# Level products of a chunked decay and of a triangular inverse on 64 of 128 columns

## The chip, the cores and the metric

The program runs on one core of a Trainium2 chip. The metric is the device time of one execution in microseconds (us); three executions were timed. TensorE multiplies 128x128 stationary weights with moving columns and writes to PSUM; VectorE and ScalarE read PSUM and SBUF; GpSimd computes only a few small powers; the sync engine issues the weight transfers. In the rows TensorE's matmuls are PE, its weight loads PEld, VectorE is DVE, ScalarE is ACT.

## The reference, cut to what matters

Two layers of a first block (attention, the HGRN2 recurrence, memory attention), then two layers of a second block (gated delta rule, pooling, retention, then a feed-forward part), on 256 positions of width 1024, all in fp32. The change touches two computations. In the first block, the decayed scores of the recurrence:

```
A = jnp.cumsum(lfc, axis=2)
diff = A[:, :, :, None, :] - A[:, :, None, :, :]
decay = jnp.exp(jnp.where(causal[:, :, None], diff, -jnp.inf))
scores = jnp.einsum('bhtd,bhtsd,bhsd->bhts', qc, decay, kc)
```

In the second block, the solution with a unit lower triangular matrix in the gated delta rule:

```
m = jnp.where(strict, jnp.einsum('bhnid,bhnjd->bhnij', k_beta, k) * decay, 0.0)
a = m + jnp.eye(CHUNK, dtype=m.dtype)
...
sol = lax.linalg.triangular_solve(a, rhs, left_side=True, lower=True, unit_diagonal=True)
```

## The kernel before, in words

Nothing schedules the work: each engine runs a list of instructions written out by hand, with semaphores between the lists. The 256 positions are two tiles `t` of 128 rows; both computations have four heads of width 128.

**Weights.** Every weight matrix is cut into units of up to four 128-row slices of 512 columns. A unit arrives by a transfer into one of four slots; ScalarE rounds it in two parts of 128x1024 (`round_weights`, line 1007), VectorE subtracts the rounded part from the original (`weight_rests`, line 1368), and TensorE multiplies with both (`split_part`, lines 548 and 557): 24 matmuls of 512 columns for a unit. `round_until(i)` and `rests_until(i)` in the lists of ScalarE and VectorE say at which place the units up to number i are prepared. TensorE's list puts one such unit between two steps of the small computations.

**Steps.** All small products go through the four PSUM banks `mp` in one fixed order of steps (`ORDER_1`, `ORDER_2`). A step waits until the bank's last content was read (`begin`), raises `step_done`, and its reader raises `step_read`.

**Decayed scores (first block).** Per layer `hg_level(n)` computes for n = 0 to 8 and each tile four fp32 products, one for each head (line 668). For n from 1 to 7 the level stands for pairs of neighbouring runs of m = 2^(n-1) positions, and only entries whose row is in a left run and whose column is in the right run of the same pair count. VectorE's `products(n)` fills only the left runs of `kmul` and the right runs of `qmul`; ScalarE's `level_exp(n)` (lines 1073 and 1074) gives the exponentials. `collect(n)` on VectorE copies 128x512 from PSUM into `hst` under the level's mask (line 1621). TensorE's order is: level n, one weight unit, level n+1.

**Inverse (second block).** The inverse `inv` of a head's 128x128 matrix and its transpose `invT` are built level by level, m = `LEVELS[n]` = 2, 4, ..., 64 for n = 1 to 6. VectorE masks the level's part `ml` out of the matrix (`level_mask`, raises `inv_ready`). Then, for each tile and head (`quad`, line 826):

- Y = ml^T inv, copied by ScalarE into `yl` (`evacuate`, lines 1238 and 1291);
- Z = invT^T yl, which VectorE subtracts from `inv` (line 1896; not at the last level);
- W = yl^T invT, which VectorE subtracts from `invT` (line 1900).

All operands are 128x128 for each head, though a level changes only the left runs of m columns of `inv` and the right runs of `invT`. TensorE's order at a level is: Y of both tiles, one weight unit, Z of both tiles, W of both tiles, one weight unit, then what `BETWEEN` puts there (retention and pooling). ScalarE's list at the start of this stage (lines 1287 to 1311) is: take over the sums of the `DZ` unit, sigmoid of `RG`, sigmoid of `DZ`, two roundings of the next unit, the two copies of Y1, two more roundings.

```
for n, g in enumerate(("DZ", "G2", "G3", "G4", "G5", "G0", None)):
    if n < 6:
        round_until(17 + 2 * n)
    for t in range(TT if n > 0 else 0):
        evacuate(f"Y{n}_{t}", yl[:, t], bank(s(f"Y{n}_{t}"), NH, P))
```

Beside these, `attn_values` (line 722) multiplies 128x128 weights with 64 moving columns, the step `ba` (line 789) with 16, and `pool_mix` (line 872) with 256.

## Time and profile before

| | |
|---|---|
| time, median of 3 | 1568.52 us (1568.07 to 1570.97) |
| the profiled execution's own time | 1567.28 us |
| its span in the trace | 1565.5 us |
| mean granted clock of TensorE | 0.976 |
| busy: PE, PEld, DVE, ACT, POOL | 1464.9, 1228.0, 954.9, 694.9, 52.9 us |
| first block, level products | 86.6 to 140.9 us, and 344.1 to 398.3 us |
| second block, inverse | 644.6 to 765.9 us, and 1162.5 to 1283.4 us |

The span lies 1.8 us inside the time of its own execution, and that execution 1.2 us below the median of the three. Matmuls are pipelined: a busy figure of PE holds overlapping pieces, so how long a matmul holds the engine is read from the chain of waits or from the distance of the starts. An fp32 matmul of this program stands in the trace as two records, a product with rounded operands (line 548, 557, 789) as one. The granted clock is a share of 2.4 GHz; its two levels are 1.0 and 0.5.

### The profile page before, as it was taken

The page shows a single profiled execution, that of the slowest core. Times are in us where ns is not written, and L with a number is a line of the kernel's source. Part 1 is how long each engine was busy: PE and PEld are TensorE (multiplying, and loading weights), DVE is VectorE, ACT ScalarE, POOL GpSimd, SP SyncE. Part 2 cuts the span into 40 slices and gives each one's busy share as a digit, 9 for nine tenths or more (in the row PEclk, how much of TensorE's full clock was granted, in tenths as well). Part 3 has the DMA queues.
Part 4 walks back from the last instruction along what each step waited for, and adds up shares of the span by engine and source line. Part 5 has one row for each costly group of instructions (what it writes and reads, how often), then busy time and mean ns, then how long its engine had stood idle before and what let it go on. Part 6 is the DMA issues. An engine that isn't in the chain of part 4 may idle for free.

```text
span 1565.5 us, 19971 instructions
## 1 busy us (share of the span) xinstructions
PE 1464.9 (94%) x8234; PEld 1228.0 (78%) x8234; DVE 954.9 (61%) x1160; ACT 694.9 (44%) x971; POOL 52.9 (3%) x41
## 2 busy tenths in 40 slices
PE   5999878999887999999998999989999999899997
PEld 4988757888776798888554999869888866489986
DVE  7588553779763657955344566464796543366654
ACT  4754563575553457433204443344754311343332
POOL 0002000000200000000000000000000000000000
PEclk9999888999998999999999999999999999999999
DMA  7444222544322365433343565544543334445553
GB/s 257 145 152 152 72 98 81 173 151 149 121 86 77 132 208 178 135 108 108 108 161 108 188 187 178 188 147 169 188 135 108 108 108 162 134 152 179 181 176 120
DMA packets 138985, 225.79 MB, mean 144 GB/s; under 512 B 7888, under 2 KB 54288, under 8 KB 138768
## 3 DMA queue, kind: packets, MB, share of 16 engines
q1 hardware_dynamic: 133456, 221.60, 43.1%
q10 hardware_dynamic: 5440, 2.93, 0.6%
q8 instruction: 66, 1.08, 0.3%
q14 instruction: 23, 0.19, 0.0%
HBM read 223.46 MB, written 1.05 MB: 143 GB/s over the span
## 4 chain that ended last, share of the span: by engine, by line
PE 84%; DVE 7%; ACT 5%; issue 2%; POOL 1%; ACTq 0%; DMA 0%; POOLq 0%; DVEq 0%
PE gp L557 42%; PE gp L548 20%; PE gp L530 5%; PE mp L826 5%; PE gp L607 3%; PE mp L512 2%; PE mp L668 2%; DVE wt_rest L1368 2%; DVE arena L1362 1%; ACT arena L1081 1%; PE mp L722 1%; POOL rs_out L2023 1%; ACT first_hi L1007 1%; ACT arena L1238 0%; PE mp L789 0%
## 5 line engine op out<-in xcount | busy, mean ns | idle before, releaser
L1368 DVE TENSOR_TENSOR wt_rest<-wt,wt_hi 128x1024 fp32r<-128x1024 f32 x140 | 164.9, 1221 | 72.1 <-ACT wt_hi L1007 72.0
L1007 ACT ACTIVATE wt_hi<-wt 128x1024 fp32r<-128x1024 f32 x140 | 140.3, 1051 | 116.7 <-DMA wt<-in_ffn_down 60.5
L1368 DVE TENSOR_TENSOR wt_rest<-wt,mix_hi 128x1024 fp32r<-128x1024 f32 x112 | 132.5, 1221 | 56.4 <-ACT mix_hi L1007 55.6
L1368 DVE TENSOR_TENSOR wt_rest<-wt,first_hi 128x1024 fp32r<-128x1024 f32 x118 | 139.2, 1219 | 41.2 <-ACT first_hi L1007 40.5
L548 PE MATMUL gp<-hT_hi,wt_hi 128*128 128x256 f32 x576 | 163.3, 284 | 0.0
L548 PE MATMUL gp<-hT_hi,wt_rest 128*128 128x256 f32 x576 | 163.0, 283 | 0.0
L548 PE MATMUL gp<-hT_rest,wt_hi 128*128 128x256 f32 x576 | 163.0, 283 | 0.0
L557 PE MATMUL gp<-wt_rest,mix_hT_hi 128*128 128x512 f32 x384 | 153.8, 400 | 0.0
L1007 ACT ACTIVATE first_hi<-wt 128x1024 fp32r<-128x1024 f32 x118 | 121.1, 1062 | 71.4 <-PE gp L557 60.4
L557 PE MATMUL gp<-mix_hi,mix_hT_hi 128*128 128x512 f32 x352 | 142.6, 405 | 8.6 <-DVE arena L1785 5.7
L1007 ACT ACTIVATE mix_hi<-wt 128x1024 fp32r<-128x1024 f32 x112 | 114.7, 1059 | 79.5 <-PE gp L557 29.8
L557 PE MATMUL gp<-mix_hi,mix_hT_rest 128*128 128x512 f32 x352 | 137.9, 392 | 0.0
L980 ACT ACTIVATE arena<-gp 128x1024 f32<-128x1024 f32 x48 | 49.1, 1022 | 168.7 <-PE gp L557 168.7
L1362 DVE TENSOR_TENSOR arena<-arena,gp 128x512 f32<-128x512 f32 (+1 forms) x56 | 44.9, 801 | 124.4 <-ACT arena L1339 68.1
L557 PE MATMUL gp<-first_hi,first_hT_hi 128*128 128x512 f32 x256 | 105.3, 411 | 6.9 <-DVE wt_rest L1368 6.9
L548 PEld LDWEIGHTS gp<-hT_rest,wt_hi 128*128 128x128 f32 x576 | 110.6, 192 | 0.0
L548 PEld LDWEIGHTS gp<-hT_hi,wt_hi 128*128 128x128 f32 x576 | 110.5, 192 | 0.0
L548 PEld LDWEIGHTS gp<-hT_hi,wt_rest 128*128 128x128 f32 x576 | 110.5, 192 | 0.0
L1238 ACT ACTIVATE arena<-mp 128x512 f32<-128x512 f32 x84 | 46.2, 601 | 131.6 <-PE mp L826 61.3
L557 PE MATMUL gp<-wt_rest,first_hT_hi 128*128 128x512 f32 x256 | 103.8, 406 | 0.0
L2023 POOL TENSOR_TENSOR rs_out<-rs_in,minus_half 128x1 f32<-128x1 f32 (+3 forms) x37 | 52.7, 1426 | 1506.5 <-DVE rs_in L1373 1506.5
L557 PE MATMUL gp<-first_hi,first_hT_rest 128*128 128x512 f32 x256 | 103.0, 402 | 0.0
(290 smaller groups left out, 3086.3 us busy)
## 6 DMA issues: line engine op xcount, KB each, us to landing
wt<-in_w_in SPq DMA_DIRECT2D x100, 1024.0 KB, 5.0
wt<-in_ffn_gate SPq DMA_DIRECT2D x44, 512.0 KB, 4.0
wt<-in_ffn_up SPq DMA_DIRECT2D x44, 512.0 KB, 5.0
wt<-in_w_out SPq DMA_DIRECT2D x20, 1024.0 KB, 5.0
wt<-in_ffn_down SPq DMA_DIRECT2D x20, 1024.0 KB, 5.0
wt<-in_w_mem_kv SPq DMA_DIRECT2D x8, 1024.0 KB, 5.1
wt<-in_w_branch_pool SPq DMA_DIRECT2D x4, 1024.0 KB, 5.1
wt<-in_w_branch_ret SPq DMA_DIRECT2D x4, 1024.0 KB, 5.0
```

The lines of the kernel that those rows point to most:

```text
L512: last = nc.tensor.transpose(bank(step)[:, P * j:P * j + P], tile, ident)
L530: last = nc.tensor.matmul(group_bank(group, t), stationary(k0 + k, t), wt[:, u % SLOTS, k, :], start=(k0 + k == 0), stop=(k0 + k == GROUPS ...
L548: last = nc.tensor.matmul(o, a[:, k, P * c:P * c + P], b[:, :, k0 + k, :], start=(k0 + k == 0 and c % 2 == 0 and i == 0), stop=(k0 + k == ...
L557: last = nc.tensor.matmul(group_bank(group, t), a, b[:, k, :], start=(kk == k_first and i == 0), stop=(kk == k_last and i == 2))
L607: last = nc.tensor.matmul(group_bank(GROUPS[g][0], t), stationary(k0 + k, t), wt[:, u % SLOTS, k, :], start=(k0 + k == 0), stop=(k0 + k == ...
L826: last = nc.tensor.matmul(bank(step)[:, P * h:P * h + P], lhs(h), rhs(h), start=True, stop=True)
L980: nc.scalar.activation(dst, group_banks(name), func).then_inc(group_read[GROUP_NO[name] % 2], 1)
L1007: nc.scalar.activation(rounded_part(u)[:, k:k + nk, :], wt[:, u % SLOTS, k:k + nk, :], ACT.Copy)\
L1238: nc.scalar.activation(dst, src, ACT.Copy, scale=scale).then_inc(step_read[STEP_NO[s(step)] % 4], 1)
L1362: return nc.vector.tensor_tensor(o, i0, i1, ALU.mult)
L1368: return nc.vector.tensor_tensor(o, i0, i1, ALU.subtract)
L2023: nc.gpsimd.tensor_tensor(rs_out[:, at:at + width], rs_in[:, at:at + width], minus_half[:, 0:width], ALU.pow)\
```

## The change

Of each head only the 64 columns that a level changes are moved through TensorE and copied. The moving operand is a view of runs of m with gaps of m; the 4 x 64 columns of a step lie packed in the first half of its PSUM bank. VectorE's copies and subtractions and ScalarE's copies of Y take 256 elements and write them into runs. The weights of each matmul stay 128x128. W uses all 128 columns of `yl` as weights, so those that Y no longer writes have to be zero: there are now two buffers `yls`, used in turn (one where the masked decay was, which is free once step `at1` was read). ScalarE sets both to zero behind the sigmoid of `DZ`, and after the Y copies of levels 2 to 5 it clears the right runs of the other buffer for the next level.

```diff
         decT, mT, atT = (region(b_c + 1024 * i, TT, NH, P) for i in range(3))
-        inv, invT, yl = (region(b_e + 1024 * i, TT, NH, P) for i in range(3))
+        inv, invT = (region(b_e + 1024 * i, TT, NH, P) for i in range(2))
+        yls = [region(at_, TT, NH, P) for at_ in (b_c, b_e + 2048)]
...
+
+        def blocks(v, m, right):
+
+            return v.rearrange("p (b m) -> p b m", m=2 * m)[:, :, m:] if right else v.rearrange("p (b m) -> p b m", m=2 * m)[:, :, 0:m]
+
+        def head_blocks(v, m, right):
+
+            z = v.rearrange("p h (b m) -> p (h b) m", m=2 * m)
+            return z[:, :, m:] if right else z[:, :, 0:m]
+
+        def half_bank(step, m):
+
+            return bank(step, NH * P // 2 // m, m)
+
+        def half_head(step, h, m):
+            return bank(step)[:, P // 2 * h:P // 2 * (h + 1)].rearrange("p (b m) -> p b m", m=m)
...
                         begin(s(f"hg{n}_{t}"), (sig("hg_factors"), 9 * l + n + 1))
                         kt = t if n < 8 else 0
                         for h in range(NH):
-                            last = nc.tensor.matmul(bank(s(f"hg{n}_{t}"))[:, P * h:P * h + P], src_k[:, h, kt * P:kt * P + P],
-                                                    src_q[:, h, t * P:t * P + P], start=True, stop=True)
+                            later = src_q[:, h, t * P:t * P + P]
+                            if 0 < n < 8:
+                                m = 2 ** (n - 1)
+                                o, later = half_head(s(f"hg{n}_{t}"), h, m), blocks(later, m, True)
+                            else:
+                                o = bank(s(f"hg{n}_{t}"))[:, P * h:P * h + P]
+                            last = nc.tensor.matmul(o, src_k[:, h, kt * P:kt * P + P], later, start=True, stop=True)
                         end(last)
...
+
+                def half_quad(step, m, lhs, rhs, *waits):
+                    begin(step, *waits)
+                    for h in range(NH):
+                        last = nc.tensor.matmul(half_head(step, h, m), lhs(h), rhs(h), start=True, stop=True)
+                    end(last)
                 for n in range(1, len(LEVELS)):
-                    for t in range(TT):
-                        quad(s(f"Y{n}_{t}"), lambda h: ml[:, t, h, :], lambda h: inv[:, t, h, :], (sig("inv_ready"), len(LEVELS) * l + n + 1))
+                    m, yl = LEVELS[n], yls[n % 2]
+                    for t in range(TT):
+                        half_quad(s(f"Y{n}_{t}"), m, lambda h: ml[:, t, h, :], lambda h: blocks(inv[:, t, h, :], m, False),
+                                  (sig("inv_ready"), len(LEVELS) * l + n + 1))
                     if n < len(LEVELS) - 1:
                         filler()
                         for t in range(TT):
-                            quad(s(f"Z{n}_{t}"), lambda h: invT[:, t, h, :], lambda h: yl[:, t, h, :], read_out(s(f"Y{n}_{t}")))
+                            half_quad(s(f"Z{n}_{t}"), m, lambda h: invT[:, t, h, :], lambda h: blocks(yl[:, t, h, :], m, False), read_out(s(f"Y{n}_{t}")))
                     else:
                         for i in range(2):
                             pe.wait_ge(*read_out(s(f"py{i}")))
                         branch("BP0", from_pool)
                     for t in range(TT):
-                        quad(s(f"W{n}_{t}"), lambda h: yl[:, t, h, :], lambda h: invT[:, t, h, :], read_out(s(f"Y{n}_{t}")))
+                        half_quad(s(f"W{n}_{t}"), m, lambda h: yl[:, t, h, :], lambda h: blocks(invT[:, t, h, :], m, True), read_out(s(f"Y{n}_{t}")))
                     filler()
...
                 for n, g in enumerate(("DZ", "G2", "G3", "G4", "G5", "G0", None)):
                     if n < 6:
                         round_until(17 + 2 * n)
+                    if n > 0:
+                        act.wait_ge(sig("yl_clear"), 6 * l + max(2, n))
                     for t in range(TT if n > 0 else 0):
-                        evacuate(f"Y{n}_{t}", yl[:, t], bank(s(f"Y{n}_{t}"), NH, P))
+                        evacuate(f"Y{n}_{t}", head_blocks(yls[n % 2][:, t], LEVELS[n], False), half_bank(s(f"Y{n}_{t}"), LEVELS[n]))
+                    if 2 <= n < 6:
+                        m = LEVELS[n + 1]
+                        odd = head_blocks(yls[(n + 1) % 2].rearrange("p t h i -> p (t h) i"), m, True)
+                        nc.scalar.activation(odd, odd, ACT.Copy, scale=0.0).then_inc(sig("yl_clear"), 1)
                     if n < 5:
                         round_until(18 + 2 * n)
                     if g is not None:
...
                         nc.scalar.activation(region(b_x, TT, G), reg("B", "RG"), ACT.Sigmoid).then_inc(sig("out_sig"), 1)
                         act.wait_ge(*taken(s("DZ")))
                         nc.scalar.activation(region(b_x + 1024, TT, G), reg("B", "DZ"), ACT.Sigmoid).then_inc(sig("out_sig"), 1)
+                        act.wait_ge(*read_out(s("at1")))
+                        for yl in yls:
+                            nc.scalar.activation(yl.rearrange("p t h i -> p (t h) i"), upper[:, None, :].to_broadcast([P, TT * NH, P]), ACT.Copy, scale=0.0)                                .then_inc(sig("yl_clear"), 1)
...
                         mask = (ident if n == 0 else level[:, n - 1, :]).bitcast(mybir.dt.uint32)
-                        evac(nc.vector.copy_predicated(hst[:, t], mask[:, None, :].to_broadcast([P, NH, P]), bank(st, NH, P)), st)
+                        if n == 0:
+                            evac(nc.vector.copy_predicated(hst[:, t], mask[:, None, :].to_broadcast([P, NH, P]), bank(st, NH, P)), st)
+                            continue
+                        m = 2 ** (n - 1)
+                        pairs = P // 2 // m
+                        evac(nc.vector.copy_predicated(hst[:, t].rearrange("p h (b m) -> p h b m", m=2 * m)[:, :, :, m:],
+                                                       blocks(mask, m, True)[:, None].to_broadcast([P, NH, pairs, m]),
+                                                       bank(st)[:, 0:NH * P // 2].rearrange("p (h b m) -> p h b m", h=NH, m=m)), st)
...
                         for t in range(TT):
                             st = s(f"Z{n}_{t}")
                             dve.wait_ge(*computed(st))
-                            evac(sub(inv[:, t], inv[:, t], bank(st, NH, P)), st)
+                            here = head_blocks(inv[:, t], LEVELS[n], False)
+                            evac(sub(here, here, half_bank(st, LEVELS[n])), st)
                     for t in range(TT if n > 0 else 0):
                         st = s(f"W{n}_{t}")
                         dve.wait_ge(*computed(st))
-                        evac(sub(invT[:, t], invT[:, t], bank(st, NH, P)), st)
+                        here = head_blocks(invT[:, t], LEVELS[n], True)
+                        evac(sub(here, here, half_bank(st, LEVELS[n])), st)
```

**ScalarE at the start of the inverse,** second block, layer 0, before: from the sum of `DZ` (line 980) to the copies of Y2. Rows of 128x1024 from `wt` are roundings; `x2` means twice in a row.

```order
L1298 ACT_TABLE_LOAD
L1298 ACTIVATE arena<-arena 128x1024
L1300 ACTIVATE arena<-arena 128x1024
L1007 ACTIVATE mix_hi_55<-wt 128x1024 x2
L1238 ACTIVATE arena<-mp 128x512 x2
L1007 ACTIVATE mix_hi_54<-wt 128x1024 x2
L980 ACTIVATE arena<-gp 128x1024
L1238 ACTIVATE arena<-mp 128x512 x4
L1007 ACTIVATE mix_hi_55<-wt 128x1024 x2
L1238 ACTIVATE arena<-mp 128x512 x2
```

The same place with the change (its lines lie some 30 to 40 further down):

```order
L1334 ACT_TABLE_LOAD
L1334 ACTIVATE arena<-arena 128x1024
L1336 ACTIVATE arena<-arena 128x1024
L1339 ACTIVATE arena<-const 128x1024 x2
L1037 ACTIVATE mix_hi_55<-wt 128x1024 x2
L1268 ACTIVATE arena<-mp 128x128x2 x2
L1037 ACTIVATE mix_hi_54<-wt 128x1024 x2
L1010 ACTIVATE arena<-gp 128x1024
L1268 ACTIVATE arena<-mp 128x512 x4
L1037 ACTIVATE mix_hi_55<-wt 128x1024 x2
L1268 ACTIVATE arena<-mp 128x64x4 x2
L1327 ACTIVATE arena<-arena 128x64x8
```

Two clears of 128x1024 (line 1339) now stand ahead of the two roundings and the copies of Y1; the copies of a level write 128x128x2, 128x64x4 and so on for 128x512; the first clear of half a buffer (line 1327) stands behind the copies of Y2.

**TensorE between the first two levels,** before: the last rows of the weight unit behind Y1, Z1 and W1 together (line 826), and the first of the next unit.

```order
L557 MATMUL gp<-mix_hi_54,mix_hT_rest 128x512
L557 MATMUL gp<-mix_hi_54,mix_hT_hi 128x512
L557 MATMUL gp<-wt_rest,mix_hT_hi 128x512
L557 MATMUL gp<-mix_hi_54,mix_hT_rest 128x512
L826 MATMUL mp<-arena 128x128 x16
L557 MATMUL gp<-mix_hi_55,mix_hT_hi 128x512
```

With the change:

```order
L574 MATMUL gp<-mix_hi_54,mix_hT_rest 128x512
L574 MATMUL gp<-mix_hi_54,mix_hT_hi 128x512
L574 MATMUL gp<-wt_rest,mix_hT_hi 128x512
L574 MATMUL gp<-mix_hi_54,mix_hT_rest 128x512
L917 MATMUL mp<-arena 128x64 x16
L574 MATMUL gp<-mix_hi_55,mix_hT_hi 128x512
```

Nothing changes place on TensorE: the same 16 products stand there, with 64 columns for 128.

**VectorE at level 1 of the inverse,** before: the two weight rests, the four subtractions of Z1 and W1, the mask of level 2, the next rests.

```order
L1362 TENSOR_TENSOR arena<-arena,const 128x16x64
L1365 TENSOR_TENSOR arena<-arena 128x16x64
L1368 TENSOR_TENSOR wt_rest<-wt,mix_hi_55 128x1024 x2
L1368 TENSOR_TENSOR arena<-arena,mp 128x512 x4
L1362 TENSOR_TENSOR arena<-arena,const 128x1024
L1368 TENSOR_TENSOR wt_rest<-wt,mix_hi_54 128x1024 x2
```

With the change:

```order
L1401 TENSOR_TENSOR arena<-arena,const 128x16x64
L1404 TENSOR_TENSOR arena<-arena 128x16x64
L1407 TENSOR_TENSOR wt_rest<-wt,mix_hi_55 128x1024 x2
L1407 TENSOR_TENSOR arena<-arena,mp 128x128x2 x4
L1401 TENSOR_TENSOR arena<-arena,const 128x1024
L1407 TENSOR_TENSOR wt_rest<-wt,mix_hi_54 128x1024 x2
```

Only the shape of the subtractions changes, not their place.

## Rows read from the trace of the kernel before

**Rows 1.** The page's fourth part: shares of the chain that ended last.

```profile
PE 84%; DVE 7%; ACT 5%; issue 2%; POOL 1%; ACTq 0%; DMA 0%; POOLq 0%; DVEq 0%
```

**Rows 2.** Chain, first block: start us, length us, engine, tile, line, records.

```profile
86.61 1.78 PE mp L668 x16
...
152.90 0.88 PE mp L682 x4
```

**Rows 3.** Chain of waits, the inverse in layer 0 of the second block.

```profile
651.50 1.78 PE mp L826 x16
...
658.88 3.57 PE mp L826 x32
...
744.21 1.73 PE mp L872 x8
...
765.90 0.03 issue
```

**Rows 4.** Chain of waits, matmuls with 64 and with 16 moving columns.

```profile
242.25 5.32 PE mp L722 x48
...
552.88 4.09 PE mp L789 x32
```

**Rows 5.** Groups by shape: line, engine, operation, shape, count; busy us, mean ns.

```profile
L826 PE MATMUL mp<-arena 128*128 128x128 f32 x656 | 78.3, 275 | 0.0
...
L722 PE MATMUL mp<-arena 128*128 128x64 f32 x96 | 10.9, 274 | 0.0
```

**Rows 6.** Order of time, ScalarE: start us, length us, line, operation, count.

```profile
654.84 1.04 ACT L1300 ACTIVATE arena<-arena 128x1024 f32<-128x1024 f32 x1
655.79 1.99 ACT L1007 ACTIVATE mix_hi<-wt 128x1024 fp32r<-128x1024 f32 x2
657.68 1.07 ACT L1238 ACTIVATE arena<-mp 128x512 f32<-128x512 f32 x2
...
672.83 1.12 ACT L1238 ACTIVATE arena<-mp 128x512 f32<-128x512 f32 x2
...
1175.21 1.07 ACT L1238 ACTIVATE arena<-mp 128x512 f32<-128x512 f32 x2
```

**Rows 7.** Order of time, TensorE's weight loads (PEld) and matmuls (PE) around Z.

```profile
658.50 3.77 PEld L826 LDWEIGHTS mp<-arena 128*128 128x128 f32 x32
...
658.72 3.73 PE L826 MATMUL mp<-arena 128*128 128x128 f32 x32
...
676.93 3.77 PEld L826 LDWEIGHTS mp<-arena 128*128 128x128 f32 x32
...
1176.03 3.77 PEld L826 LDWEIGHTS mp<-arena 128*128 128x128 f32 x32
```

**Rows 8.** Order of time, VectorE: behind the level products, and at level 1.

```profile
148.47 1.22 DVE L1673 TENSOR_REDUCE small<-arena 128x16 f32<-128x1024 f32 x1 [2.94 <-ACT arena L1150]
...
660.18 2.18 DVE L1368 TENSOR_TENSOR arena<-arena,mp 128x512 f32<-128x512 f32 x3
```

**Rows 9.** Groups by shape, VectorE and ScalarE.

```profile
L1621 DVE COPY_PREDICATED arena<-const,mp 128x512 f32<-128x512 uint32 x32 | 23.6, 737 | 0.6
...
L1260 ACT ACTIVATE arena<-gp,cols 128x256 f32<-128x256 f32 x24 | 9.3, 470 | 0.0
```

**Rows 10.** Order of time, a ScalarE copy for which TensorE waits.

```profile
773.96 0.60 ACT L1238 ACTIVATE arena<-mp 128x512 f32<-128x512 f32 x1 [5.53 <-PE mp L826]
...
774.70 0.46 PE L922 MATMUL mp<-arena 128*128 128x128 f32 x2 [0.78 <-ACT arena L1238]
775.00 0.39 PE L923 MATMUL mp<-arena 128*128 128x128 f32 x2
```

**Rows 11.** Stretches: busy us of each engine, then granted clock, DMA share, GB/s.

```profile
242.00:247.50 5.50, 5.50 (x50) 5.37 (x48) 0.69 (x1) 1.06 (x1) 0.00 (x0) 1.00 0.57 191
248.40:255.10 6.70, 4.08 (x10) 3.25 (x11) 5.84 (x5) 0.00 (x0) 0.00 (x0) 0.50 0.00 0
...
555.60:562.30 6.70, 6.70 (x33) 6.70 (x33) 3.81 (x10) 3.40 (x6) 0.00 (x0) 0.50 0.64 253
```

## The prediction

> **What bounds the kernel now.** I read the page's shares of the chain first, then the chain in order of time through the two stages that the change touches, then the groups of matmuls kept apart by shape, and last the order of time on ScalarE and TensorE around the inverse. The page puts 84% of the chain on TensorE [rows 1]: a gain must come out of TensorE's stream or out of a wait of TensorE. In the forget-gate stage the chain never leaves TensorE from the first level product at 86.61 us to the memory scores at 152.90 us [rows 2]; the second block's stage has the same pattern. In the inverse it stays on TensorE from 651.50 to 765.90 us, through all levels [rows 3]. So what VectorE and ScalarE do there is hidden for as long as it is in time.
>
> **Part 1, TensorE: 64 columns for 128.** In the forget gate 7 levels x 2 tiles x 4 heads x 2 blocks = 112 matmuls shrink; in the inverse Y 48, Z 40 and W 48 per block, 272 in both. The profile records an fp32 matmul twice (the 164 matmuls per block of line 826 are 656 records [rows 5]), so 384 matmuls are 768 records. How long does a record hold the engine? From the chain: level products 1.78 us for 16 records, 0.111 us each [rows 2]; inverse 3.57 us for 32, 0.112 us [rows 3]. The attention values of line 722 have exactly the new shape, 128x128 weights and 64 moving columns: 5.32 us for 48 records, 0.111 us each [rows 4]. With 16 columns (line 789, at full clock for about its first half) the engine is no quicker either: 4.09 us for 32, 0.128 us [rows 4]. With 256 columns a record does grow: 1.73 us for 8, 0.216 us [rows 3]. So columns set the pace down to 128; below that something costs 0.111 us whatever moves, and the one thing that these matmuls share is a load of 128 weight columns ahead of each record, which the change leaves as it is. Saved: 768 x (0.112 - 0.111), below 1 us, taken as **zero**. Bounds: 44 us saved if the pace followed the columns all the way down (a quarter of the 0.216 us is 0.054; 768 x 0.058), zero by the row of the same shape, and the shape decides.
>
> The page "TensorE: Matmul & The Clock Gate" of the Trainium skill gives, in its section on the back-to-back issue gap, N/2.4 + 2.5 ns for an isolated matmul; by that alone, twice per record, a record would fall from 112 to 58 ns and the kernel to about 1527 us. Its section on LDWEIGHTS says P/1.2 ns for P weight columns, 107 ns for 128, whatever moves; by that rule nothing is won, and line 722 sides with this one.
>
> The moving operand is now read in runs of m elements with gaps of m. No row shows such a read by TensorE. Since 128 columns also fit into 0.112 us, a read at half speed stays hidden: cost zero, my value. At a quarter of the speed a record would take the 0.216 us of 256 columns, the upper bound and a rival below.
>
> **Part 2, VectorE.** 28 predicated copies of 737 ns [rows 9] and 44 subtractions (three of them take 2.18 us [rows 8]) now handle 256 elements for 512. If each lost at most its half, that is 10 us and 16 us of VectorE. I price it at zero: TensorE is the cover, gap-free across both stages [rows 2, 3]. After the level products VectorE sits idle for 2.94 us at 148.47 us because ScalarE waits for a weight group of TensorE [rows 8], so an earlier VectorE only waits longer. The mask product for the next inverse level is needed only behind the 24 matmuls of a weight unit. A slower strided access would have the same cover.
>
> **Part 3, ScalarE, the part that costs.** Y copies: 24 of 0.60 us [rows 10] become 24 of between 0.30 (half) and 0.47 us (a 128x256 copy out of PSUM with a column scale [rows 9]); I take 0.42, nearer the shape that is there. Added: per block four clears of 512 elements behind the Y copies of levels 2 to 5, and two clears of 1024 elements **ahead of the copies of Y1**. The four take some 0.6 us each, less what the copies ahead of them save, and Z has room there: the copies of Y2 end at 672.83 + 1.12 = 673.95, Z2 begins at 676.93 [rows 6, 7]. Zero. The two clears are different. From 654.84 on ScalarE runs without a break: a sigmoid, two roundings at 655.79, the copies of Y1 from 657.68 to 658.75 [rows 6]. TensorE's weight load for Z1_0, which needs the first of these copies, starts at 658.50, and its matmul at 658.72 [rows 7], while that copy ends at about 658.28. **The slack is 0.2 us.** The clears go in at 655.79. One 1024-element operation occupies ScalarE for 0.95 us start to start (654.84 to 655.79), two for 1.90. So the Y1 copy starts at 657.68 + 1.90 = 659.58 and ends at 659.58 + 0.42 = 660.00. From the end of such a copy to the waiting matmul pass 0.14 us (774.56 to 774.70 [rows 10]), and the first pair after a pause takes some 0.07 us more than 0.22 (774.70 to 775.00 in the same stretch, 0.30). TensorE resumes at 660.14, as if at 660.21, instead of 658.72: 1.49 us. Z1_1 needs the second copy, about 0.35 us behind the first, and is itself 0.9 us behind Z1_0: nothing more. Block 2 has the same picture, 1175.21 against 1176.03 [rows 6, 7]. What else stands behind the clears: the two roundings, now done at 655.79 + 1.90 + 1.99 = 659.68, and VectorE's two rests after each, done by about 661.3; TensorE wants that unit behind W1, at 658.88 + 3.57 [rows 3] + 1.5 = 663.9. In time. With a copy of 0.30 or 0.47 and clears of 0.9 to 1.05 the pause is 1.3 to 1.8. **Two pauses: +3.0 us (2.5 to 3.6).** Downstream TensorE meets no wait that could take the delay back before 765.90 [rows 3], and the waits after that are for work that follows from its own.
>
> **Part 4, the clock.** In the trace of before the 64-column run at 242 to 247.5 us keeps 2.4 GHz, but right after its end, with TensorE idle for under a microsecond, the granted clock is 0.50, 1.2 GHz, from 248.4 to 255.1. After about three microseconds of 16-column matmuls without any pause it is 0.50 too, from 555.6 to 562.3 [rows 11]. [...] The change puts a 1.5 us pause in front of 3.6 us of half-filled matmuls. If the clock falls there, 3.4 to 6.7 us at half speed cost 1.7 to 3.4 us per block, 3.4 to 6.7 us in both. No row has this mixture. Dense units stand on both sides of it, as they do not in the two rows, so I take 0.4 us, near the low end, and keep 6.7 for the range.
>
> **Sum.** 0 + 0 + 3.0 + 0.4 = +3.4 us. The profiled execution took 1567.28 us (span 1565.5), 1.24 us below the median of 1568.52; 1567.28 + 3.4 = 1570.7 for it, **1571.9 us** against the median.
>
> **The rivals.**
> - Pause and falling clock together: 3.0 + 3.4 to 6.7, 1575 to 1578 us. For it: the two rows on sparse streams. Against: the pause is short, and the unit ahead of it is dense.
> - The columns set TensorE's pace after all: 44 us less, 3.0 more, 1527 us, the side of faster. It decides from the point where a 64-column record takes less than 0.108 us (768 x 0.004 pays for the pauses). For it: 256 columns cost twice 128. Against: line 722.
> - The gapped moving read is slow: 80 records per block have m of 1 or 2 (32 in the gate, 48 in the inverse), 160 x (0.216 - 0.112) = 17 us, 1588 us at the worst, 1580 if half of it. No row excludes it; that every VectorE operation in the same patterns keeps its time speaks against.
> - The cost is not there: the clears are cheaper or ScalarE starts earlier, so Z1 waits for under 0.5 us: 1568.5 to 1569.5. Against: slack of 0.2 us against 1.9.
>
> **How the numbers follow.** Forecast (pause, clock as good as untouched, 1570.9 to 1572.3): 0.55. Pause and clock: 0.25. Cost absent: 0.10. Slow gapped read: 0.05. Columns pay, wholly or in part: 0.05. The range leaves out the last two and the tip of the clock case: 1568.3 to 1577. A measurement tells about 0.2%, 3.1 us, from no change; the pause alone, 3.0, stands right at that bound. So the forecast's 0.55 splits into 0.29 within and 0.26 slower; slower is 0.26 + 0.25 + 0.05 = 0.56, within 0.29 + 0.09 = 0.38, faster 0.06.
>
> **What would show it.** Right: 64-column records still 0.111 to 0.112 us apart; ScalarE's two clears of about 1 us ahead of two roundings and the Y1 copies; TensorE idle for about 1.4 us before Z1 in each block, released by the Y copy; VectorE's idle time up by what its operations lose. Wrong: a chain in which 16 level records take under 1.7 us, or over 1.9 at small m; no idle time before Z1; or granted clock 0.50 inside the inverse, which moves the time to the first rival.

## The result and the profile after

Seven executions of the changed kernel had a median of 1578.01 us (1572.53 to 1581.22), seven of the kernel before, on the same chip, 1568.64 us (1567.29 to 1571.85). The ratio is 1.0048, 95% interval 1.0031 to 1.0065: **slower by 0.48%**. Against the median of 1568.52 us that the forecast started from, the ratio gives 1576.0 us. It lies in the upper end of the range of 1568.3 to 1577.0, 4 us above the number itself, while the plain median, 1578.0, lies above the range: the quotient of the two medians would be 1.0060, above the ratio on record but inside its interval.

The profiled execution is one of the quicker ones: 1573.16 us, span 1571.3 (before 1567.28 and 1565.5), mean granted clock 0.971 (0.976). The page, busy time of each engine and the shares of the chain:

```profile
PE 1469.3 (94%) x8234; PEld 1231.7 (78%) x8234; DVE 938.3 (60%) x1160; ACT 697.7 (44%) x983; POOL 52.8 (3%) x41
...
PE 83%; DVE 7%; ACT 6%; issue 3%; POOL 1%; ACTq 0%; DMA 0%; POOLq 0%; DVEq 0%
```

VectorE has lost 16.6 us of its 954.9, ScalarE gained 2.8, and TensorE, for which 384 matmuls move half the columns, shows 4.4 us **more**. In the chain ScalarE and issue have one point each more than before [rows 1].

The new shapes, groups kept apart by shape (line, engine, operation, shape, count; busy us, mean ns; idle time before them and its releaser):

```profile
L917 PE MATMUL mp<-arena 128*128 128x64 f32 x544 | 65.6, 278 | 2.5 <-ACT arena L1268 2.5
L691 PE MATMUL mp<-arena 128*128 128x64 f32 x224 | 26.5, 271 | 0.0
...
L1407 DVE TENSOR_TENSOR arena<-arena,mp 128x256 f32<-128x256 f32 x44 | 18.6, 422 | 69.9 <-PE mp L917 69.6
L1665 DVE COPY_PREDICATED arena<-const,mp 128x256 f32<-128x256 uint32 x28 | 14.6, 521 | 2.9 <-PE mp L691 2.5
...
L1268 ACT ACTIVATE arena<-mp 128x256 f32<-128x256 f32 x24 | 8.4, 389 | 6.3 <-PE mp L917 6.3
L1327 ACT ACTIVATE arena<-arena 128x512 f32<-128x512 f32 x8 | 5.2, 648 | 0.0
L1339 ACT ACTIVATE arena<-const 128x1024 f32<-128x1024 f32 x4 | 4.0, 1042 | 0.0
```

The inverse's 272 matmuls are 544 records of 64 columns and still 278 ns each in the records (275 before [rows 5]); the gate's 224 are at 271. A subtraction takes 422 ns, a predicated copy 521 for 737 [rows 9]. The one idle time of TensorE in these lines is 2.5 us ahead of line 917, ended by the Y copies of ScalarE.

The chain of waits of the changed kernel, the inverse of the first of its two layers, in order of time (start us, length us, engine, tile, line, records):

```profile
644.18 5.59 PE gp L574 x24
...
654.14 1.90 ACT arena L1339 x2
...
657.83 0.39 ACT arena L1268
...
658.35 5.64 PE mp L917 x32
663.99 6.94 PE gp L574 x24
670.93 1.75 PE mp L529 x16
...
680.18 3.52 PE mp L917 x32
683.70 5.66 PE gp L574 x24
```

Before, this stretch never left TensorE [rows 3]. Now it goes over ScalarE: its two clears (line 1339), two roundings, the first copy of Y1, and then Z1. Two things differ from the levels further down: Z1 and W1 (658.35) take 5.64 us where Z2 and W2 (680.18) take 3.52, and the unit behind them takes 6.94 where the later one takes 5.66. The windows of the same trace say why (stretch, busy us and instructions of PE, PEld, DVE, ACT, POOL, then granted clock, DMA share, GB/s):

```profile
650.00:659.80 9.80, 8.57 (x51) 7.18 (x51) 8.82 (x8) 9.77 (x12) 0.00 (x0) 1.00 0.47 144
660.00:666.60 6.60, 6.60 (x26) 6.02 (x26) 3.28 (x5) 0.36 (x1) 0.00 (x0) 0.50 0.24 92
...
1185.00:1195.00 10.00, 10.00 (x65) 8.77 (x64) 5.57 (x6) 3.21 (x6) 0.00 (x0) 1.00 0.26 82
```

From 660.0 to 666.6 us TensorE runs at the lower of its levels, 1.2 GHz; at the same place of the second layer it keeps 2.4 GHz.

**Where the time went, by the chain.** I take it from the start of the unit ahead of Y1 to the end of the unit behind W1. Before: it begins a unit of 5.6 us ahead of 651.50, at 645.9, and ends at 658.88 + 3.57 + 5.6 = 668.05 [rows 3], 22.2 us. After, first layer: 644.18 to 670.93, 26.75 us. In the second layer of the same trace, where the clock holds, the piece takes 23.6 us, from the first of these lines to the second:

```profile
1168.18 5.59 PE gp L574 x24
...
1191.76 1.75 PE mp L529 x16
```

So the pause costs 1.4 us per layer and the fall of the clock 26.75 - 23.6 = 3.2 us. Two pauses and one fall are 6.0 us; the spans differ by 5.8. That the two agree is in part chance: outside the inverse the changed kernel's trace has 85 us at half clock for 75 before, it reaches the first piece 1.7 us earlier than the kernel before and loses 1.9 us between the two pieces.

The order of time of ScalarE around the pause (start us, length us, line, operation, count; idle time before it in brackets):

```profile
653.09 1.04 ACT L1336 ACTIVATE arena<-arena 128x1024 f32<-128x1024 f32 x1
654.04 1.99 ACT L1339 ACTIVATE arena<-const 128x1024 f32<-128x1024 f32 x2
655.94 1.99 ACT L1037 ACTIVATE mix_hi<-wt 128x1024 fp32r<-128x1024 f32 x2
657.83 0.66 ACT L1268 ACTIVATE arena<-mp 128x256 f32<-128x256 f32 x2
```

It is the row of before [rows 6] with the clears pushed in: sigmoid at 653.09, clears 0.95 us later, roundings 1.90 us later still, and the Y1 copies 4.74 us behind the sigmoid for 2.84.

### The profile page after: what moved, and what is told of

It is laid out like the page before. It is cut to its first block, busy times and chain, and to the rows that moved or that the text cites. A ratio compares the mean times of both kernels' runs of the same rounds, so it can differ in the third digit from the quotient of the medians.

```text
span 1571.3 us, 19995 instructions
## 1 busy us (share of the span) xinstructions
PE 1469.3 (94%) x8234; PEld 1231.7 (78%) x8234; DVE 938.3 (60%) x1160; ACT 697.7 (44%) x983; POOL 52.8 (3%) x41
## 3 DMA queue, kind: packets, MB, share of 16 engines
q8 instruction: 66, 1.08, 0.3%
## 4 chain that ended last, share of the span: by engine, by line
PE 83%; DVE 7%; ACT 6%; issue 3%; POOL 1%; ACTq 0%; DMA 0%; POOLq 0%; DVEq 0%
PE gp L574 41%; PE gp L565 20%; PE gp L547 5%; PE mp L917 4%; PE gp L624 3%; PE mp L529 2%; PE mp L691 2%; DVE wt_rest L1407 2%; DVE arena L1401 1%; PE mp L848 1%; ACT arena L1111 1%; PE mp L744 1%; POOL rs_out L2071 1%; ACT first_hi L1037 1%; ACT arena L1268 1%
## 5 line engine op out<-in xcount | busy, mean ns | idle before, releaser
L1268 ACT ACTIVATE arena<-mp 128x512 f32<-128x512 f32 (+1 forms) x84 | 41.1, 541 | 132.8 <-PE mp L529 59.1
```

The source lines that it names most:

```text
L1268: nc.scalar.activation(dst, src, ACT.Copy, scale=scale).then_inc(step_read[STEP_NO[s(step)] % 4], 1)
```

## The experiments

All ratios are against the kernel before, run on the same chip at the same time. Edits are shown against the kernel named ahead of them.

**The changed kernel again.**

> The changed kernel once more, as the yardstick on this chip. My theory (a pause of TensorE of 1.4 us ahead of Z1 in both layers, and a fall of the clock there in a part of the executions): 6 to 11 us over before, executions in two clusters, about 4 and about 10 us over it. The rival that the pause alone is the cost (3 us): under 4 us over before in all of them.

Measured: 1578.50 us against 1569.65, ratio 1.0058 (1.0037 to 1.008). The size is as expected, the two clusters are not there: the eight times spread from 1574.8 to 1583.2 us without a gap. Now the clock falls in both layers. Windows of this second trace of the changed kernel:

```profile
664.30:671.00 6.70, 6.70 (x28) 6.22 (x28) 3.05 (x6) 0.62 (x1) 0.00 (x0) 0.50 0.27 106
...
1190.00:1196.50 6.50, 6.50 (x26) 5.93 (x26) 3.12 (x5) 0.38 (x1) 0.00 (x0) 0.50 0.24 94
```

So the fall is no accident of the one trace, and it comes behind the same pause each time. It can come in one layer or in both.

**The clears alone**, in the kernel before: all products, copies and subtractions at full width.

```diff
+                    if n > 0:
+                        act.wait_ge(sig("yl_clear"), 2 * l + 2)
...
+                        act.wait_ge(*read_out(s("at1")))
+                        for z in (decT, yl):
+                            nc.scalar.activation(z.rearrange("p t h i -> p (t h) i"), upper[:, None, :].to_broadcast([P, TT * NH, P]), ACT.Copy, scale=0.0).then_inc(sig("yl_clear"), 1)
```

> The kernel before with nothing added but the two 128x1024 clears on ScalarE at the same place; all products and copies keep 128 columns. Copies of Y1 stay at 0.6 us, so the pause is 1.90 - 0.2 + 0.14 us, about 1.7 us per layer. If the clock falls because a pause meets half-filled matmuls: no fall here, +3.4 us (2.8 to 4). If the pause alone makes it fall: +7 to 10 us as in the change. If the pause is not the cause of the loss at all: no difference.

> The kernel before with the two clears alone, all products at 128 columns, a second time. If the pause alone never brings the clock down: mean granted clock 0.9715 to 0.9725 and +2.5 to +3.5 us. If the pause is enough in some executions: clock 0.969 to 0.970 and +5 us or more.

Measured: 1573.84 us against 1569.65, ratio 1.0020 (1.0005 to 1.0035), and 1576.00 against 1569.36, ratio 1.0036 (1.0023 to 1.005). In both traces Z1 waits in both layers for the Y1 copy. The second trace, waits of TensorE in the first layer's inverse (who waits, for whom: us in total, times, longest), and then its chain:

```profile
PE mp L826 <- ACT arena L1238: 1.4, 1, 1.4
```

```profile
662.56 0.58 ACT arena L1238
...
663.28 3.81 PE mp L826 x32
667.09 5.58 PE gp L557 x24
```

Here the pause is there, 1.4 us for the 1.2 of the changed kernel since the full copy takes 0.58 for 0.39, and Z1 and W1 run at full clock behind it, in all four layers of the two traces. **The clears explain a slowdown on their own, but not all of it.** By the chain they cost 1.6 us per layer (23.8 us for the piece that took 22.2), 3.2 in all. The second reading answers neither expectation: the mean granted clock, 0.9714, is nearly that of a pause that never brings the clock down, the time, 5.2 us over before by the means, is that of one that does in some executions.

**The clears early**: the changed kernel, complete, with the two clears moved on ScalarE ahead of the takeover of `DZ`, into a stretch where it is idle while TensorE runs the last unit before Y1.

```diff
+                    if n == 0:
+                        act.wait_ge(*read_out(s("at1")))
+                        for yl in yls:
+                            nc.scalar.activation(yl.rearrange("p t h i -> p (t h) i"), upper[:, None, :].to_broadcast([P, TT * NH, P]), ACT.Copy, scale=0.0)\
+                                .then_inc(sig("yl_clear"), 1)
...
-                        act.wait_ge(*read_out(s("at1")))
-                        for yl in yls:
-                            nc.scalar.activation(yl.rearrange("p t h i -> p (t h) i"), upper[:, None, :].to_broadcast([P, TT * NH, P]), ACT.Copy, scale=0.0).then_inc(sig("yl_clear"), 1)
```

> The change with its two first clears moved ahead of the takeover of DZ, into ScalarE's idle stretch of 5.3 us; nothing is left out. My theory: no wait of TensorE ahead of Z1, no fall of the clock, the time of before within 1 us, since 64-column records hold TensorE as long as 128-column ones. If the columns or the gapped reads cost or save something of their own, it shows here by itself: slow reads +8 to +17 us, columns that pay -10 us and more.

Measured: 1569.99 us against 1569.65, ratio 1.0006 (0.9991 to 1.0022). Chain of this kernel, which has no step on ScalarE any more:

```profile
652.91 5.63 PE gp L574 x24
658.54 3.52 PE mp L917 x32
662.06 5.64 PE gp L574 x24
```

All narrow products, copies and subtractions are in it, and the four small clears too. The time is that of the kernel before within the interval: what is left of the change brings nothing, and costs nothing that this run can tell from zero. It is the best version of this edit, and it beats nothing.

**One clear ahead**: the changed kernel with the second matrix cleared behind Y1's copies, so that one clear of 0.95 us stands ahead of them. It was run twice.

```diff
-                        act.wait_ge(sig("yl_clear"), 6 * l + n)
+                        act.wait_ge(sig("yl_clear"), 6 * l + max(2, n))
...
+                    if n == 1:
+                        nc.scalar.activation(yls[0].rearrange("p t h i -> p (t h) i"), upper[:, None, :].to_broadcast([P, TT * NH, P]), ACT.Copy, scale=0.0).then_inc(sig("yl_clear"), 1)
...
-                        for yl in yls:
+                        for yl in yls[1:]:
```

> The change with only the buffer of level 1 cleared ahead of the copies of Y1, the other one behind them. The pause shrinks by one operation of 0.95 us, from 1.4 to about 0.5 us per layer: +1.0 us without a fall of the clock, which such a short pause should not bring. If the time does not follow the length of the pause (a cause elsewhere): as the change, +6 to 11.

> The kernel with one of the two clears behind Y1's copies, run a second time. The first reading was 3.5 us over the kernel before (ratio 1.0016, 1.0 to 1.0033) where its trace shows a wait of Z1 of only 0.3 us per layer and no stretch at half clock in the inverse. If the wait is all of its cost: +0.6 to +1.5 us. If a fall of the clock comes even behind so short a wait in some executions: +2.5 to +4 us again, and its trace may show one.

Measured: 1573.10 us against 1569.65, ratio 1.0016 (1.0 to 1.0033), then 1569.93 against 1570.03, ratio 1.0000 (0.9985 to 1.0014). The waits of TensorE in the second trace:

```profile
PE mp L917 <- ACT arena L1268: 0.3, 1, 0.3
```

A clear less takes 0.9 us off the wait, as the sum has it (0.95). In neither trace is there a fall of the clock in the inverse. The first reading was higher than the wait allows, the second lower; 24 executions together have a mean of 1571.2 us, 1.2 above the mean of the kernel before (1569.9, 104 executions), where two waits of 0.3 us and two slower stretches behind them (3.76 us for 3.57) make 1 us.

**The gate alone**: the changed level products and predicated copies of the forget gate, with the inverse as before.

> Only the forget gate's part of the change (64 moving columns, predicated copies of 256 elements); the inverse as before. My theory: TensorE's records stay 0.112 us apart and its stream has no gap there, so the time of before within 1 us, VectorE's idle time behind the level products up by what the copies lose. If columns set the pace: -12 us (224 records x 0.054).

Measured: 1569.66 us against 1568.34, ratio 0.9999 (0.998 to 1.0017). Chain of this kernel in the gate:

```profile
93.77 1.73 PE mp L680 x16
95.50 5.64 PE gp L563 x24
```

A level takes 1.73 + 5.64 = 7.37 us, before 1.78 + 5.59 (chain of before, 93.97 and 95.76): the 0.05 us that a level's 16 records save is in the unit behind it, so nothing is won. The records themselves still start 0.111 to 0.113 us apart, but for the first two of a level, which start 0.058 apart: that is the 0.05. The level of blocks of one element, the one shown, has the same 1.73 us as the others.

**Fewer weight columns**, in the forget gate alone: the weights of a level product are half a matrix, 64 columns. Both kernels leave out the products of the other 64 rows, so they tell what a record costs and are no versions of the program. The first has the gate's 64 moving columns and predicated copies too; its edit is shown against the kernel of the gate alone.

```diff
-                            last = nc.tensor.matmul(o, src_k[:, h, kt * P:kt * P + P], later, start=True, stop=True)
+                            half = 0 < n < 8
+                            last = nc.tensor.matmul(o[0:P // 2] if half else o, src_k[:, h, kt * P:kt * P + (P // 2 if half else P)], later,
+                                                    start=True, stop=True)
```

The second has nothing but the narrow weights, against the kernel before:

```diff
-                            last = nc.tensor.matmul(bank(s(f"hg{n}_{t}"))[:, P * h:P * h + P], src_k[:, h, kt * P:kt * P + P],
+                            half = 0 < n < 8
+                            rows = P // 2 if half else P
+                            last = nc.tensor.matmul(bank(s(f"hg{n}_{t}"))[0:rows, P * h:P * h + P], src_k[:, h, kt * P:kt * P + rows],
```

> As e4, and the weights of levels 1 to 7 are cut to 64 columns too; the products of the other 64 rows are left out. If the load of the weight columns is the floor of 0.112 us, it halves with them, and 64 moving columns then fit: 0.056 us per record, 224 records: about -12 us, less where VectorE or ScalarE then becomes the one that is waited for. If the floor is a fixed price of a record: no change.

> The kernel before with the weights of levels 1 to 7 cut to 64 columns (the products of the other 64 rows are left out) and 128 moving columns. If a record takes the longer of its weight load and its stream: 0.107 to 0.112 us still, no change. If the weight load alone sets the pace: 0.056 us, -12 us as in e5.

Measured: with 64 weight and 64 moving columns 1562.69 us against 1568.34, ratio 0.9957 (0.9941 to 0.9973); with 64 weight and 128 moving columns 1574.53, ratio 1.0032 (1.0016 to 1.0047). The chains, first with 64 moving columns:

```profile
92.29 1.08 PE mp L681 x16
93.37 5.78 PE gp L563 x24
```

and with 128:

```profile
94.47 1.89 PE mp L670 x16
96.36 5.78 PE gp L557 x24
```

Only where both are halved do the records come closer: their starts lie 0.058 us apart for 0.112. With 128 weight and 64 moving columns they lie 0.112 apart, with 64 and 128 it is 0.109: the larger of weight columns and moving columns sets the pace. The page "TensorE: Matmul & The Clock Gate" of the Trainium skill has P/1.2 ns for P weight columns in its section on LDWEIGHTS; by estimates from it 107 for 128 and 53 for 64. The section on the back-to-back issue gap on the same page of the Trainium skill has N/2.4 + 2.5 ns for N moving columns, an estimate of 112 for 128 and 58 for 64 if it is taken twice per record, as the prediction took it. Neither fits these runs by itself; the larger of the two does, 107 against 112 measured, 112 against 109, and 58 against 58.

The gain was smaller than expected, 6.7 us of 12. The step of 16 records at 0.058 would be 0.93, it is 1.08, and the unit takes 5.78 for 5.58: (1.78 - 1.08) - (5.78 - 5.58) = 0.50 us per level, 7.0 for 14. The weight loads and matmuls in the order of time show where the rest went. With 64 weight and 128 moving columns:

```profile
94.40 1.72 PEld L670 LDWEIGHTS mp<-arena 128*64 128x64 f32 x16 [0.37 <-issue]
94.40 1.96 PE L670 MATMUL mp<-arena 128*64 128x128 f32 x16
```

and before:

```profile
93.58 1.98 PEld L668 LDWEIGHTS mp<-arena 128*128 128x128 f32 x16
93.81 1.95 PE L668 MATMUL mp<-arena 128*128 128x128 f32 x16
```

At the first matmul with narrow weights the load starts together with its matmul and not 0.2 us ahead of it, and again at the first wide one (both at 96.29). With 128 moving columns this edge is all that is left, 0.11 + 0.20 us per level, 4.4 us for 14, where "no change" was expected and a ratio of 1.0032, 5 us, was measured. Why the load is not pulled ahead there, no run shows.

**Level 1 at full width**: the changed kernel, complete, with Y1, Z1 and W1 moving all 128 columns again. The copies and subtractions read the changed columns of them. It was run twice.

```diff
+                    if m == 2:
+                        for h in range(NH):
+                            last = nc.tensor.matmul(bank(step)[:, P * h:P * h + P], lhs(h), rhs(h), start=True, stop=True)
+                        end(last)
+                        return
```

> The changed kernel with the Y, Z and W products of the inverse's level 1 (the first level after the pause) back at all 128 moving columns; the copies and subtractions still read only the changed columns, the other levels, the gate and the two clears stand as in the changed kernel. Both theories: the wait of Z1 for the copies of Y1 stays, 1.2 to 1.4 us per layer, +2.5 to +3 us. Theory A, that the half-width products behind the pause are what lets the clock fall there: with dense columns from the first product on no stretch at half clock begins in the inverse, and the time is +2.5 to +3.5 us as with the clears alone. Rival B, that the pause and the products ahead of it are enough: a half-clock stretch of 6 to 7 us begins near 660 us, near 1187 us or at both, worth 3 to 3.5 us each, and the time is +6 to +10 us as for the change.

> The changed kernel with level 1 at full width, a second time. The first reading, +5.5 us (ratio 1.0036, 1.002 to 1.0053), lies between both theories; its mean granted clock over 8 executions was 0.9700, the changed kernel's over 25 executions 0.9682, the kernel before 0.9723 over 83. If the narrow first level is what lets the clock fall: clock 0.971 to 0.972 and +2.5 to +4 us. If the narrow levels behind it are enough: clock 0.968 to 0.969 and +7 to +9 us.

Measured: 1575.57 us against 1570.03, ratio 1.0036 (1.002 to 1.0053), then 1575.13 against 1569.36, ratio 1.0025 (1.0012 to 1.0038). The chain of the second trace, and the windows at the places where the changed kernel's clock falls:

```profile
665.45 3.81 PE mp L918 x32
669.26 5.61 PE gp L574 x24
```

```profile
665.40:672.00 6.60, 6.55 (x45) 6.03 (x46) 4.91 (x7) 2.06 (x3) 0.00 (x0) 1.00 0.47 157
...
1187.40:1194.00 6.60, 6.56 (x45) 6.07 (x46) 4.90 (x7) 2.04 (x3) 0.00 (x0) 1.00 0.48 159
```

The same pause of 1.2 us, full products behind it, and no fall, in four layers of two traces. The times, 5.0 us over before by the means in both sessions, stay between the two theories, and so does the mean granted clock, 0.9700 and 0.9702. The edit also makes Y1 wide, which stands a unit ahead of the pause; no run of this pause separates it from Z1 and W1.

**The changed kernel a third time**, beside the first of these.

> The changed kernel itself beside these two on the same chip. The pauses alone would give +2.5 to +3 us; with a fall of the clock in one layer +6, in both +9 to +10. Its two profiles so far show a fall in one layer and in both; expected +6 to +10 us, and a stretch at half clock from about 660 us, from about 1188 us or from both.

Measured: 1578.03 us against 1570.03, ratio 1.0047 (1.0029 to 1.0066). Its trace has the fall in the second layer only. The chain in both, first where the clock holds:

```profile
649.47 5.59 PE gp L574 x24
...
663.64 3.76 PE mp L917 x32
667.40 5.64 PE gp L574 x24
673.04 1.75 PE mp L529 x16
```

and where it falls:

```profile
1185.11 5.69 PE mp L917 x32
1190.80 6.92 PE gp L574 x24
1197.72 1.75 PE mp L529 x16
```

**All executions together.** Each execution comes with its mean granted clock; twice what it lacks to 1, times the span, is the time at half clock. The 104 executions of the kernel before come from the four sessions of these runs, the 25 of the change from two of them and from the seven of the result. Means, with the standard error of the mean:

| kernel | executions | time, us | at half clock, us | falls at Z1, layers of the traces |
|---|---|---|---|---|
| before | 104 | 1569.9 (0.3) | 86.7 (0.8) | 0 of 2 |
| change | 25 | 1577.8 (0.7) | 100.4 (1.7) | 4 of 6 |
| clears alone | 24 | 1574.4 (0.4) | 90.2 (1.5) | 0 of 4 |
| level 1 at full width | 18 | 1575.3 (0.5) | 94.1 (1.8) | 0 of 4 |
| one clear ahead | 24 | 1571.2 (0.7) | 86.8 (1.8) | 0 of 4 |
| clears early | 12 | 1570.6 (0.7) | 88.4 (3.2) | 0 of 2 |

The changed kernel spends 13.7 us more at half clock than the kernel before. At 3.2 us for a stretch of 6.8 that is 6.4 us, and with two pauses of 1.4, 9.2; 7.9 is measured. The same reckoning for the clears alone gives 1.6 + 3.2 = 4.8 for 4.5 measured. It is rough, since a stretch elsewhere in the kernel need not cost what one in the inverse does: the kernel with 64 weight and 128 moving columns in the gate, with no pause and nothing narrow in the inverse, has 93.7 us at half clock (1.8), 7.0 more than before, which with its 4.4 us of edges would make 7.7 where 4.7 is measured.

So the pause without narrow products costs 4.5 us, the narrow products without the pause 0.7 (0.7), and both together 7.9. With the first level wide again, 2.5 us (0.8) of that are gone. That the narrow products of level 1 are what lets the clock fall behind the pause is borne out by the traces, four of six layers against none of eight with a pause of 1.2 to 1.4 us and a wide level 1, and by those 2.5 us. What stays open is the rest of the level-1 kernel's cost: 5.3 us, of which the pauses are 2.8. Its half-clock time is 7.4 us above that of before, but in neither of its traces in the inverse; such stretches come and go elsewhere from one execution to the next (75 us in all in the trace of before, 105 in this kernel's second), and no run ties them to the edit. The same holds for the 1.3 us of the clears alone beyond their two pauses.

## Why the prediction was right, and where it was not

**Part 1, TensorE at zero: right.** 16 level records take 1.73 us, 0.108 each on average, and 32 take 3.52, 0.110, for 0.111 and 0.112; the units behind them give the difference back (5.64 for 5.58). With the clears early, the ratio of the whole change is 1.0006 (0.9991 to 1.0022). The row of the same shape [rows 4] decided it rightly against the 44 us of the pace by columns. The reason given, the load of 128 weight columns, was argued then and is shown now: halve those as well and a record takes 0.058 us. The gapped read cost nothing, down to blocks of one element.

**Part 2, VectorE at zero: right.** It lost 16.6 us of busy time and waited the longer. The wait at the end of the gate, 2.94 us before [rows 8], in the order of time of VectorE after:

```profile
146.79 1.22 DVE L1719 TENSOR_REDUCE small<-arena 128x16 f32<-128x1024 f32 x1 [3.76 <-ACT arena L1180]
```

**Part 3, the pause: right in place, cause and size.** The clears take 1.90 us between the sigmoid and the roundings, the Y1 copy 0.39 us (0.42 taken), from its end to the matmul pass 0.14. TensorE is idle for 1.23 us, and with a slower stretch behind it (3.76 for 3.57 before) a layer loses 1.4 us; 1.49 was the forecast. Two are 2.8 us for 3.0. The clears alone lost 1.6 per layer by their traces, with a Y1 copy of 0.58. Taking one clear away took 0.9 us off the wait. The four small clears cost nothing: the one of level 2 ends at 676.90, Z2 begins at 680.18.

**Part 4, the clock: the step that was mis-sized.** The text weighed a cost of 1.7 to 3.4 us per block against "Dense units stand on both sides of it" and took 0.4 us in all. The clock falls in four layers of six, for 6.8 us and 3.2 us of time each, so about 4 us per execution by the traces. The mechanism, its place (the narrow products behind the pause) and its bounds were named, and the first rival, pause and falling clock at 1575 to 1578 us, is what happened. It had a chance of 0.25, the forecast without it 0.55. The forecast's own 1570.9 to 1572.3 was missed; the time lies in the stated range because that kept most of the rival's cost, and not because the sum was right. What failed is the argument from the dense neighbours: the unit ahead of the pause did not hold the clock up, and the fall began about 1.5 us into Z1 (660.0 for 658.35), before the next unit could help. The two rows in hand for narrow streams [rows 11] both had half clock behind or inside them; the one argument against them had no row.

**The other rivals.** Columns pay (1527) and the slow gapped read (1580 to 1588) are excluded by the chain, the absent cost by the wait of 1.2 us in all six layers.

## What to carry to other kernels

In this kernel, halving the moving columns of a small fp32 matmul brought nothing while each one still loaded 128 weight columns; only with both halved did a record get shorter. That kernel left half of the products out, so a gain with all of them computed is not shown. Work that is added to a helper engine ahead of a copy that TensorE needs is paid in full beyond the slack, and the slack is read from two starts in the order of time (here 0.2 us); the same clears, put into that engine's idle stretch some 10 us earlier (at 645.76), are free. And a pause of 1.2 us cost more than itself where a narrow stream followed it: look there for the granted clock, in more than one trace, since here it fell in some layers and executions and not in others.

## What was not expected of the hardware

The narrow stream without the pause left the clock of the inverse alone (none of two layers, and none of four with a pause of 0.3 us), and so did the pause with a wide level 1 (none of eight). Together they brought it down for 6.8 us in four layers of six, though TensorE has no idle time from Z1 on.

A change of the weights' width between neighbouring matmuls cost time by itself: 0.11 us in a level with 64 columns and 0.20 us in the unit behind it, so that a kernel with half the weights to load in its level products ran 0.32% slower than the one before (1.0016 to 1.0047).
